# The third matrix of each expert in 16 KB runs, and up products that read every second pair of columns

## The chip, the cores and the metric

The kernel runs on one core of a Trainium2 chip. The time is that of one execution on the device, in microseconds (us), and the median of three runs is what is compared. The engines of the core are TensorE (PE; its weight loads are shown apart as PEld), VectorE (DVE), ScalarE (ACT), GpSimd (POOL) and SyncE (SP), which here issues most of the large loads. Sixteen DMA engines move data between the device's memory and the core's on-chip memory of 128 partitions.

## What is computed

One layer of a streaming encoder for 512 prompt frames and 32 frames of a running stream, 544 tokens in all: a mixer (attention and a gated delta rule), and behind it a mixture of 32 experts, of which each token takes two. The change touches the experts alone:

```python
N_EXPERTS, TOP_K, D_MODEL, D_EXPERT = 32, 2, 1024, 512
def run_block(args):
    tok, e, wt = args
    xb = x_pad[tok]
    h = jax.nn.silu(xb @ w_e1[e]) * (xb @ w_e3[e])      # 1024 x 512 each
    return (h @ w_e2[e]) * wt[:, None].astype(xb.dtype)  # 512 x 1024
```

All matrices are float32, so that each of the three is 2 MB and an expert is 6 MB.

## The kernel before, in words

The mixer comes first and takes some 740 us. The experts follow, in `expert_blocks`: one block for each of the 32 experts, each of up to 64 tokens (`SLOTS`). Tokens lie in slots; `fetch` (GpSimd) gathers their rows for a later block, `scatter` (GpSimd) writes the block's results to a table in device memory (`choice_rows`). Behind the last block the results are read back (`load_rows`, L2619, tile `y_rows`), weighted and added by VectorE (L2821, L2829) and stored.

**One block on TensorE** is `products`. `turn` transposes the gathered rows. Then for each of the first and the third matrix of the reference (`w_e1`, `w_e3`; slots `k.w1`, `k.w3`), eight steps over the 1024 inputs, two products in each (L2543): the array's columns are split in two halves of 64, and half `a` computes 256 of the 512 hidden columns for all 64 tokens. The tokens are the stationary operand, 256 columns of the matrix are the moving one. A float32 product shows as two records in the trace, so a block has 64 of them on this line, 32 for each matrix. VectorE multiplies silu of the one with the other into `hm` (L2577), TensorE transposes `hm` in two pieces, its even and its odd columns (`hm[:, c:FH:2]`, L2548), VectorE copies the result (`hT`, L2580), and L2555 multiplies with `w_e2` in four steps of 512 columns for each half.

**How the hidden columns are dealt** decides which rows of `w_e2` each partition must hold. Before, half `a` of the array takes the hidden columns 256a to 256a + 255, side by side. Behind the transposes partition n holds the columns 2n and 2n + 1 of the first half, and 256 + 2n and 257 + 2n of the second. So `load_down` (L2160) loads two runs of two rows to each partition, 8 KB each.

**How weights arrive.** Each matrix has a ring of three slots (`RING`). Two experts and then a third are loaded while the mixer ends; in the block loop `loads` (L2582 on) issues on SP, for the expert three blocks on: the first matrix when this block's products with it are done (`first`), the other one of the pair when its products are done (`up`), the down matrix when the down products are done (`down`). All go into one queue, q1. TensorE waits for each matrix before it is used.

Nothing else sets the order: each engine's program is written out by hand, with semaphores, and blocks 6 to 29 are in a loop in which each engine does the same for three blocks.

Of the kernel before, what the change touches and what calls it, by code (L numbers as in the profile page):

```python
# [147 lines left out]
def build(nc, ins, outs):  # L148
    k = Kernel(nc, ins, outs)
    k.chains = {}  # L150
    with k.top:
# [61 lines left out]
        with ExitStack() as k.experts, ExitStack() as k.rings, ExitStack() as k.routing:  # L213
            expert_tensors(k)
            k.run(project_and_choose)
            k.routing.close()
            k.run(expert_blocks)
# [1926 lines left out]
def expert_matrix(k, name, e):  # L2144
    src = k.i[name]
    return src[0, e] if isinstance(e, int) else src[0, bass.ds(e, 1)].rearrange("o r n -> (o r) n")


def load_weights(k, sp, name, tiles, loaded, e, slot):

    src = expert_matrix(k, name, e).rearrange("(p k) n -> p (k n)", p=128)
    sp.dma_start(tiles[slot][:].rearrange("p k n -> p (k n)"), src).then_inc(loaded[slot], 16)
# [6 lines left out]

def load_down(k, sp, e, slot):  # L2160

    src = expert_matrix(k, "w_e2", e).rearrange("(a p b) n -> p a (b n)", a=2, p=128)
    sp.dma_start(k.w2[slot][:].rearrange("p (a b) n -> p a (b n)", a=2), src).then_inc(k.w2_loaded[slot], 16)


def project_and_choose(k):
# [21 lines left out]
    with nc.Block() as block:  # L2188
        @block.sync
        def _(sp):  # L2190
            for j in (2 * KD - 2, 2 * KD - 1):
                o.load(sp, j)
            sp.wait_ge(padded, 2)
            load_router(k, sp)
            for e in range(RING - 1):
                load_up(k, sp, e, e)
                load_down(k, sp, e, e)
            sp.wait_ge(projected, 2)
            load_weights(k, sp, "w_e1", k.w1, k.w1_loaded, RING - 1, RING - 1)
            sp.wait_ge(projected, 4)  # L2200
            load_weights(k, sp, "w_e3", k.w3, k.w3_loaded, RING - 1, RING - 1)
            sp.wait_ge(projected, 5)
            load_down(k, sp, RING - 1, RING - 1)
# [237 lines left out]
def expert_blocks(k):  # L2441
# [4 lines left out]
    nc = k.nc  # L2446
    V = nc.vector
    FH, NF = FE // 2, FE // 128
    STEPS, EARLY = NE // RING, 2 * RING
    further = -(-NT // SLOTS)  # L2450
    with ExitStack() as ctx:
# [4 lines left out]
        xT = k.sb("b_xT", [128, KD, SLOTS], F32, ctx)  # L2456
# [26 lines left out]
        sl = (lo, hi)  # L2483
# [3 lines left out]
        def wait(eng, sem, value):  # L2487

            if not isinstance(value, int) or value > 0:
                eng.wait_ge(sem, value)  # L2490
# [23 lines left out]
        def turn(pe, b, slot, n):  # L2514
            pe.wait_ge(gathered[slot], 16 * n + 16)
            wait(pe, copied, 2 * b)

            nc.tensor.matmul(X[0][:, 0:64], xg[lo, slot, 0:128], k.ident[lo, lo], start=True, stop=True)  # L2518
            nc.tensor.transpose(X[1][:, 0:64], xg[hi, slot, 0:128], k.ident[hi, hi])
            for d in range(1, 4):  # L2520
                for a in range(2):
                    last = nc.tensor.transpose(X[a][:, 64 * d:64 * d + 64], xg[sl[a], slot, 128 * d:128 * d + 128],  # L2522
                                               k.ident[sl[a], sl[a]])
            return last

        def place_first(pe):
# [3 lines left out]
            last.then_inc(placed, 1)  # L2530
            pe.wait_ge(joined, 1)

        def products(pe, b, slot, n, prev):
            turn(pe, b, slot, n).then_inc(turned, 1)
            pe.wait_ge(copied, 2 * b + 1)
            wait(pe, hidden, b)
            for bank, w, loaded, made in ((1, k.w1, k.w1_loaded, first), (2, k.w3, k.w3_loaded, up)):
                pe.wait_ge(loaded[slot], 16 * n + 16)
                for d in range(KD):
                    if bank == 1 and d == 4:  # L2540
                        pe.wait_ge(copied, 2 * b + 2)
                    for a in range(2):
                        last = nc.tensor.matmul(k.bank[bank][sl[a], 0:FH], xT[:, d, :], w[slot][:, d, FH * a:FH * a + FH],  # L2543
                                                start=(d == 0), stop=(d == KD - 1))
                last.then_inc(made, 1)
            pe.wait_ge(hidden, b + 1)
            for c in range(2):
                last = nc.tensor.transpose(k.bank[3][:, 128 * c:128 * c + 128], hm[:, c:FH:2], k.ident[:])  # L2548
            last.then_inc(hturned, 1)
            pe.wait_ge(hcopied, b + 1)  # L2550
            pe.wait_ge(k.w2_loaded[slot], 16 * n + 16)
            wait(pe, out, b)
            for f in range(NF):
                for a in range(2):
                    last = nc.tensor.matmul(k.bank[4][sl[a], :], hT[:, f % 2, sl[f // 2]],  # L2555
                                            k.w2[slot][:, f, 512 * a:512 * a + 512], start=(f == 0), stop=(f == NF - 1))
            last.then_inc(down, 1)
# [24 lines left out]
        def loads(sp, e, b, slot, prev):  # L2582
            sp.wait_ge(first, prev + 1)
            load_weights(k, sp, "w_e1", k.w1, k.w1_loaded, e, slot)
            sp.wait_ge(up, prev + 1)
            load_weights(k, sp, "w_e3", k.w3, k.w3_loaded, e, slot)
            sp.wait_ge(down, prev + 1)
            load_down(k, sp, e, slot)
# [34 lines left out]
        with nc.Block() as block:  # L2623
# [61 lines left out]
            @block.tensor  # L2685
            def _(pe):
                def beside(b):
                    if b == NE - 2:
                        pe.wait_ge(last_made, 1)
                        for t, (c0, n) in enumerate(TILES):  # L2690
                            place = k.bank[6][:, 128 * (t - 1):128 * t] if t else k.bank[7][:, 0:NS]
                            last = nc.tensor.transpose(place, last_oh[0:n, t, :], k.ident[0:n, 0:n])
                        last.then_inc(last_turned, 1)
                    if b != 4:
                        return
                    pe.wait_ge(coded, 1)
                    for m in range(10):
                        j = m // 5
                        last = nc.tensor.matmul(M[:, MORE * j:MORE * j + MORE], r1[:, m, :], b1[:, m, :],
                                                start=(m == 0), stop=(m == 9))  # L2700
                    last.then_inc(listed, 1)

                place_first(pe)
                n = run_blocks(pe, products, beside)
                pe.wait_ge(last_kept, 1)
                pe.wait_ge(out, n + NE)
                for m, t in enumerate(ORDER):
                    rows = TILES[t][1]
                    if m == 4:
                        pe.wait_ge(finished, 2)  # L2710
                    for a in range(2):
                        last = nc.tensor.matmul(END[m][a][0:rows, :], last_rows[sl[a], t, 0:rows], y[sl[a], (NE - 1) % RING, :],
                                                start=True, stop=True)
                    last.then_inc(last_in, 1)
# [142 lines left out]
```

## Time and profile before

| | us |
|---|---|
| median of three runs | 1228.68 |
| lowest and highest run | 1225.5, 1230.6 |
| the profiled execution | 1229.07 |
| its span, first to last instruction | 1227.3 |
| TensorE busy with products | 1090.4 (89%) |
| VectorE, ScalarE, GpSimd busy | 430.4, 354.9, 389.0 |
| moved by DMA | 284.58 MB, of it 244.94 MB on queue q1 |
| granted TensorE clock, mean | 0.958 |

TensorE is busy for 89% of the span, but that is a mean over the mixer and the experts, and the two have different limits. The page's strip of 40 slices shows the DMA engines at 20 to 70% up to 660 us, and at 90% or more, with 424 to 429 GB/s, from 767 us to almost the end. Shares of the whole run thus don't say what an edit in the experts is worth; the stretch from 740 us on has to be read by itself.

### The profile page before, as it was taken

How to read it: one execution, taken by the hardware profiler on the slowest of the kernel's cores; microseconds unless marked ns; L12 is line 12 of the kernel's file. 1: busy time of each engine (PE TensorE's matmuls, PEld its weight loads, DVE VectorE, ACT ScalarE, POOL GpSimd, SP SyncE). 2: the span in 40 equal slices, each digit the busy share in tenths (PEclk: the TensorE clock that was granted, in tenths of full speed). 3: DMA queues.
4: the chain of work that ended last, by engine and by line, in shares of the span. 5: the costliest groups of instructions: out<-in, count | busy, mean ns of one | idle time of the engine just before them, and what ended most of it. 6: DMA issues, size and time to landing. Idle time of an engine off the chain costs nothing. (4 is left out here: it accounts for less than half of the span.)

```text
span 1227.3 us, 20556 instructions
## 1 busy us (share of the span) xinstructions
PE 1090.4 (89%) x8243; PEld 834.8 (68%) x8243; DVE 430.4 (35%) x987; ACT 354.9 (29%) x749; POOL 389.0 (32%) x426
## 2 busy tenths in 40 slices
PE   5999899899999989999999898888888888777884
PEld 4998888798998868888898764454444444444441
DVE  6697733881111454331333442321111111111116
ACT  6547634352222735543332531000000000000000
POOL 4554468841212442332563102112121122111100
PEclk9999999898999989999999877998999999999997
DMA  7332236255322611115331985999999999999996
GB/s 130 87 87 61 69 93 170 43 171 142 91 69 71 222 55 52 53 49 183 93 95 36 369 323 214 427 426 429 426 428 429 427 428 429 427 427 429 429 428 263
DMA packets 149146, 284.58 MB, mean 232 GB/s; under 512 B 43588, under 2 KB 118948, under 8 KB 132688
## 3 DMA queue, kind: packets, MB, share of 16 engines
q1 hardware_dynamic: 93696, 244.94, 51.5%
q10 hardware_dynamic: 49632, 27.46, 8.3%
q0 software_dynamic: 5744, 11.15, 2.4%
q8 instruction: 51, 0.84, 0.3%
q14 instruction: 23, 0.19, 0.0%
HBM read 267.08 MB, written 24.31 MB: 237 GB/s over the span
## 5 line engine op out<-in xcount | busy, mean ns | idle before, releaser
L2543 PE MATMUL bank<-e_w,b_xT 128*64 128x256 f32 x2048 | 236.1, 388 | 33.2 <-DMA e_w<-in_w_e 17.6
L490 PE MATMUL bank<-xhi,cv_w_hi 128*128 128x272 f32 x848 | 258.1, 304 | 8.3 <-PEq L134 2.6
L476 POOL TENSOR_TENSOR cv_w_lo<-cv_w_raw,cv_w_hi 128x1024 fp32r<-128x1024 f32 (+1 forms) x69 | 166.8, 2418 | 305.8 <-ACT cv_w_hi L469 289.6
L490 PE MATMUL bank<-xhi,cv_w_lo 128*128 128x272 f32 x848 | 249.0, 294 | 0.0
L490 PE MATMUL bank<-xlo,cv_w_hi 128*128 128x272 f32 x848 | 248.4, 293 | 0.0
L2543 PEld LDWEIGHTS bank<-e_w,b_xT 128*64 128x64 f32 x2048 | 149.6, 139 | 109.6 <-DVE b_xT L2572 26.2
L490 PEld LDWEIGHTS bank<-xhi,cv_w_hi 128*128 128x128 f32 x848 | 163.7, 193 | 17.0 <-issue 9.7
L490 PEld LDWEIGHTS bank<-xlo,cv_w_hi 128*128 128x128 f32 x848 | 164.1, 194 | 1.1
L490 PEld LDWEIGHTS bank<-xhi,cv_w_lo 128*128 128x128 f32 x848 | 163.8, 193 | 0.0
L2555 PE MATMUL bank<-e_w,b_hiddenT 128*64 128x512 f32 x512 | 118.6, 605 | 20.7 <-DVE b_hiddenT L2580 20.7
L2507 POOL COPY b_target<-slot_target 128x1 int32 (+1 forms) x31 | 5.6, 180 | 327.3 <-ACT b_y L2565 327.3
L2565 ACT ACTIVATE b_y<-bank 128x512 f32<-128x512 f32 x32 | 19.1, 597 | 286.5 <-PE bank L2555 286.5
L2577 DVE TENSOR_TENSOR b_hidden<-b_silu,bank 128x256 f32<-128x256 f32 x32 | 13.5, 422 | 243.5 <-issue 233.7
L2555 PEld LDWEIGHTS bank<-e_w,b_hiddenT 128*64 128x64 f32 x512 | 36.9, 138 | 80.4 <-issue 53.9
L469 ACT ACTIVATE cv_w_hi<-cv_w_raw 128x1024 fp32r<-128x1024 f32 (+1 forms) x69 | 69.3, 1004 | 28.4 <-DMA cv_w_raw<-in_w_br_a 16.5
L2572 DVE TENSOR_TENSOR b_xT<-bank,g_ffn_runs 128x256 f32<-128x256 f32 x64 | 24.2, 419 | 129.0 <-PE bank L2522 128.1
L678 DVE SCALAR_TENSOR_TENSOR conv_acc<-conv_in,wconv,conv_acc 128x547 f32<-128x547 f32 x48 | 60.5, 1261 | 1.7
L2562 ACT ACTIVATE b_silu<-bank 128x256 f32<-128x256 f32 x32 | 12.3, 383 | 144.2 <-PE bank L2543 144.2
L2075 PE MATMUL bank<-o_hi,mix_prompt 128*128 128x512 f32 x128 | 44.3, 411 | 1.4 <-PEq L134 0.7
L490 PE MATMUL bank<-yb_hi,cv_w_hi 128*128 128x272 f32 x128 | 41.4, 324 | 1.4 <-DVE yb_lo L1648 1.4
L490 PE MATMUL bank<-yb_lo,cv_w_hi 128*128 128x272 f32 x128 | 38.4, 300 | 0.0
L490 PE MATMUL bank<-yb_hi,cv_w_lo 128*128 128x272 f32 x128 | 38.4, 300 | 0.0
(447 smaller groups left out, 1650.7 us busy)
## 6 DMA issues: line engine op xcount, KB each, us to landing
e_w<-in_w_e SPq DMA_DIRECT2D x96, 2048.0 KB, 28.9
cv_w_raw<-in_w_in ACTq DMA_DIRECT2D x34, 512.0 KB, 4.1
cv_w_raw<-in_w_in SPq DMA_DIRECT2D x18, 512.0 KB, 3.9
cv_w_raw<-in_w_br_b ACTq DMA_DIRECT2D x8, 512.0 KB, 4.2
o_raw<-in_w_out SPq DMA_DIRECT2D x16, 256.0 KB, 3.6
y_rows<-choice_rows SPq DMA_DIRECT2D x8, 512.0 KB, 7.3
g_values_gates<-g_z_stage ACTq DMA_DIRECT2D x12, 272.0 KB, 4.6
f_gates<-g_values_gates SPq DMA_DIRECT2D x2, 1088.0 KB, 11.1
```

What stands on the lines that cost most here:

```text
L469: self.k.nc.scalar.activation(self.whi[:, c % OPS, 0:nk, :], self.raw[:, c % RAWS, 0:nk, :], ACT.Copy)\
L476: self.k.nc.gpsimd.tensor_tensor(self.wlo[:, s, 0:nk, :], self.raw[:, s, 0:nk, :], self.whi[:, c % OPS, 0:nk, :].bitcast(F32), ALU.subtract)\
L490: last = self.k.nc.tensor.matmul(self.bank(c, h)[:, 0:HALF], w, x[:, d, cols], start=(d == 0 and n == 0), stop=(d == nk - 1 and n == 2))
L678: op = nc.vector.scalar_tensor_tensor(out=ac[:, 0:W], in0=ci[:, w:w + W], scalar=k.wconv[:, w, c:c + 1], in1=ac[:, 0:W], op0=ALU.mult, op1 ...
L2075: last = k.nc.tensor.matmul(bank[0:n, :], rows, w[:, d, :], start=(start and i == 0), stop=(d == KD - 1 and i == 2))
L2507: nc.gpsimd.tensor_copy(to[:, slot:slot + 1], k.dst[:, bass.ds(column, 1)]).then_inc(aimed, 1)
L2543: last = nc.tensor.matmul(k.bank[bank][sl[a], 0:FH], xT[:, d, :], w[slot][:, d, FH * a:FH * a + FH], start=(d == 0), stop=(d == KD - 1))
L2555: last = nc.tensor.matmul(k.bank[4][sl[a], :], hT[:, f % 2, sl[f // 2]], k.w2[slot][:, f, 512 * a:512 * a + 512], start=(f == 0), stop=(f ...
L2562: nc.scalar.activation(act[:], k.bank[1][:, 0:FH], ACT.Silu).then_inc(silu, 1)
L2565: nc.scalar.activation(y[:, slot, :], k.bank[4][:], ACT.Copy).then_inc(out, 1)
L2572: nc.vector.tensor_tensor(xT[:, f], X[a][:, 0:4 * SLOTS].rearrange("p (k s) -> p k s", k=4), k.gain[:, f].unsqueeze(2).broadcast_to([128, ...
L2577: nc.vector.tensor_tensor(hm[:], act[:], k.bank[2][:, 0:FH], ALU.mult).then_inc(hidden, 1)
```

## The change

Two things that belong together. Half `a` of the array no longer takes 256 hidden columns side by side, but the columns 4n + 2a and 4n + 2a + 1 for each n from 0 to 127: pairs, dealt to the halves in turn. The moving operand of L2543 is read with a step for that: two floats (8 bytes), then two left out. The number of columns, of products and of steps is the same. Behind the transposes partition n then holds the hidden columns 4n to 4n + 3, so that its rows of `w_e2` are four neighbours, one run of 16 KB, and `load_down` becomes the same call as for the other two matrices.

```diff
 def load_down(k, sp, e, slot):

-    src = expert_matrix(k, "w_e2", e).rearrange("(a p b) n -> p a (b n)", a=2, p=128)
-    sp.dma_start(k.w2[slot][:].rearrange("p (a b) n -> p a (b n)", a=2), src).then_inc(k.w2_loaded[slot], 16)
+    load_weights(k, sp, "w_e2", k.w2, k.w2_loaded, e, slot)
...
+        def pairs_of(row, a):
+
+            return row.rearrange("p (n f) -> p n f", f=NF)[:, :, 2 * a:2 * a + 2]
+
...
-                        last = nc.tensor.matmul(k.bank[bank][sl[a], 0:FH], xT[:, d, :], w[slot][:, d, FH * a:FH * a + FH],
+                        last = nc.tensor.matmul(k.bank[bank][sl[a], 0:FH], xT[:, d, :], pairs_of(w[slot][:, d, :], a),
                                                 start=(d == 0), stop=(d == KD - 1))
```

No instruction moves to another place. On SP, at the place where the first loads of expert weights are issued (the end of the mixer; `e_w_0_8390`, `8391` and `8392` are the first, third and down matrix of ring slot 0, the next three those of slot 1), the change reads:

```order
 L2152 DMA e_w_0_8390<-in_w_e 128x4096
 L2152 DMA e_w_0_8391<-in_w_e 128x4096
-L2163 DMA e_w_0_8392<-in_w_e 128x2x2048
+L2152 DMA e_w_0_8392<-in_w_e 128x4096
 L2152 DMA e_w_1_8393<-in_w_e 128x4096
 L2152 DMA e_w_1_8394<-in_w_e 128x4096
-L2163 DMA e_w_1_8395<-in_w_e 128x2x2048
+L2152 DMA e_w_1_8395<-in_w_e 128x4096
 L2152 DMA e_w_2_8396<-in_w_e 128x4096 [waits g_last]
```

The down load keeps its place and its waits and loses a dimension of its pattern. The other engines' programs read alike but for line numbers.

## Rows read from the trace of the kernel before

**Rows 1.** The chain that ended last: start us, us, what; the first blocks.

```profile
744.20 9.98 PE bank L2543 x64
...
760.56 3.70 PE bank L2543 x32
...
774.08 3.70 PE bank L2543 x32
```

**Rows 2.** The same chain later, up to its end.

```profile
983.83 3.70 PE bank L2543 x32
...
997.29 3.70 PE bank L2543 x32
1001.14 37.77 DMA e_w<-in_w_e
...
1039.05 3.69 PE bank L2543 x32
1042.89 42.20 DMA e_w<-in_w_e
...
1085.23 3.69 PE bank L2543 x32
...
1177.67 3.69 PE bank L2543 x32
...
1181.77 4.50 issue
...
1193.19 6.55 DMA choice_rows<-b_y,b_target
...
1203.78 10.64 DMA y_rows<-choice_rows
```

**Rows 3.** Windows: stretch, length, busy (count) by engine, PEclk, DMA share, GB/s.

```profile
770.00:1000.00 230.00, 200.72 (x1525) 108.42 (x1523) 38.77 (x110) 16.28 (x33) 47.95 (x102) 0.99 1.01 427
1000.00:1180.00 180.00, 145.36 (x1092) 81.69 (x1090) 19.21 (x48) 11.76 (x24) 31.93 (x67) 0.99 1.01 428
```

**Rows 4.** DMA queues, whole run: packets, MB, share of 16 engines' time.

```profile
q1 hardware_dynamic: 93696, 244.94, 51.5%
```

**Rows 5.** The same queue from 1000 to 1180 us alone.

```profile
q1 hardware_dynamic: 6534, 73.92, 96.4%
```

**Rows 6.** Line L2163, the down loads: ns min/median/max of the issue.

```profile
L2163 SPq DMA_DIRECT2D e_w<-in_w_e x32: 378/384/4415, 677.7 to 1161.5; - x32
```

**Rows 7.** Timeline of TensorE: one block while the ring is ahead.

```profile
916.54 7.13 PE L2543 MATMUL bank<-e_w,b_xT 128*64 128x256 f32 x64 [0.53 <-DVE b_xT L2572]
```

**Rows 8.** Timeline late: products with idle time before them and releaser.

```profile
1177.67 3.67 PE L2543 MATMUL bank<-e_w,b_xT 128*64 128x256 f32 x32 [0.74 <-DMA e_w<-in_w_e]
...
1182.49 3.67 PE L2543 MATMUL bank<-e_w,b_xT 128*64 128x256 f32 x32 [1.15 <-DMA e_w<-in_w_e]
...
1193.45 3.67 PE L2543 MATMUL bank<-e_w,b_xT 128*64 128x256 f32 x32 [0.61 <-DVE b_xT L2572]
```

**Rows 9.** Timeline at 62 us: mixer products, float32r, contiguous moving operand.

```profile
62.04 0.29 PE L490 MATMUL bank<-xhi,cv_w_hi 128*128 128x272 f32 x1
62.16 0.29 PE L490 MATMUL bank<-xlo,cv_w_hi 128*128 128x272 f32 x1
62.29 0.29 PE L490 MATMUL bank<-xhi,cv_w_lo 128*128 128x272 f32 x1
```

**Rows 10.** Weight loads of lines L2548 and L2699: ns min/median/max.

```profile
L2548 PEld LDWEIGHTS bank<-ident,b_hidden x64: 194/205/219, 754.8 to 1202.0; 128*128 128x128 f32 x64
...
L2699 PEld LDWEIGHTS bank<-m_blk_oh,m_rank_oh x20: 186/192/192, 813.4 to 815.5; 128*128 128x128 f32 x20
```

**Rows 11.** Line L2510, the 31 scatters: issue to landing.

```profile
DMA to landing us min/median/max: 6.5/7.8/8.9
```

**Rows 12.** A window in which the stream ran fastest: TensorE columns, PEclk, DMA share, GB/s.

```profile
1043.80:1047.50 3.70, 3.63 (x32) 2.21 (x32) 1.00 1.06 440
```

## The prediction

> **What bounds the kernel now.** I read the chain that ended last first, since the engines' shares mix the mixer with the experts. Both edits lie behind 740 us. In the first blocks the chain goes through TensorE and the small copies beside it alone: the products of block 1 start at 760.56, of block 2 at 774.08 [rows 1], and and blocks 17 and 18 at 983.83 and 997.29, a period of 13.46 us [rows 2]. In this stretch TensorE doesn't wait for weights, because three experts were loaded before it began. From block 18 on the chain is different: the products with one matrix (3.69 us) and then 42.20 us of a weight load, over and over [rows 2]. A load is issued when its slot comes free and lands 42 us later, since eight other matrices stand ahead of it in the queue. Blocks 21 and 30 start at 1039.05 and 1177.67, so nine blocks take 138.6 us, 15.40 us each [rows 2].
>
> The windows then say why: the DMA engines are at a share of 1.01, with 427 GB/s, from 770 to 1000 us already, and at 428 GB/s from 1000 to 1180 [rows 3]. The stream of weights is full from the first released slot on; TensorE, at 13.46 us a block, only lives on the lead of the ring until block 18. Check: q1 moves 73.92 MB in 180 us [rows 5], which is 0.411 MB/us, and an expert's 6.29 MB take 15.3 us by that, which is the 15.40 of the chain. So **the experts' stretch is bound by the bytes and packets of the weight stream**, and behind it by a short tail: the last but one block's results go out (6.55 us) and everything is read back (10.64 us) [rows 2].
>
> TensorE's reserve is needed below. From 997.29 thirteen more blocks at 13.46 us would start block 31 at 1172.3; it starts at 1193.45 [rows 8]. So TensorE has 21.2 us in hand by then, 0.68 us a block over 31 blocks, and 1.9 us a block (15.40 less 13.46) once the lead is used up.
>
> **The change, part one: the down loads in packets of 16 KB.** The bytes stay the same. An 8 KB run is a packet, and so is a 16 KB run: a down matrix goes from 256 packets to 128, for each of 16 DMA engines from 16 to 8. What is a packet worth beyond its bytes? Two rows of the same queue give it. The whole run: 51.5% of 16 x 1227.3 us are 10113 engine-us for 244.94 MB in 93696 packets [rows 4]. The full stretch: 96.4% of 16 x 180 us are 2776 engine-us for 73.92 MB in 6534 packets [rows 5]. With a price per MB and one per packet, both rows hold for 36.4 us per MB and 12.7 ns per packet. The many small packets of the mixer (writes, and copies within device memory) carry costs of their own, so 12.7 ns is an upper end; the lower end is 0. The queue is fully busy by its share, so I see no reason for a loss here. I take the middle, 6.4 ns, as neither row shows a 16 KB packet by itself.
>
> On the path: 8 packets x 6.4 ns are 0.05 us for a down load. The chain's last load ahead of the tail is that for block 30 (TensorE idle 1.15 us before 1182.49, released by a load [rows 8]); ahead of it in the full stretch stand the down loads of experts 3 to 29, 27 of them. The five others lie before 740 us or behind. **27 x 0.05 = 1.4 us less**, and between 0 and 27 x 0.10 = 2.7 us less. The gain is not taken by what comes next: TensorE needs 13.46 us a block and would get weights each 15.35 us.
>
> The Trainium skill ("DMA: Bandwidth & Descriptors", section "Why small descriptors are slow (HBM only)") puts a fixed cost of about 3 cycles on each packet, and gives 850 MHz for the fabric. An estimate by that page is 3.5 ns a packet and 0.8 us in all; no row here shows a packet's fixed part alone.
>
> SP's own share is nothing: a down load is issued in 384 ns [rows 6] against 15.40 us a block, and nothing queued behind it on SP is late by that.
>
> **Part two: moving columns read with a step.** 1024 records on each of the two matrices' lines now read two floats of every four. The trace has no moving operand with a step, so this needs bounds. From below: nothing, or a gain of nothing, since the same columns are streamed. From above: twice the time. Three rows speak to where between. Contiguous products of 272 columns start every 0.126 us in the mixer [rows 9], 0.46 ns a column. The up products of one matrix take 3.67 us [rows 8] for 32 records of 256 columns, two at a time by the halves of the array, so 4096 columns in each stream: 0.90 ns a column. If the step halves the pace at which columns can be read, to 0.93 ns, a stream that needs 0.90 loses 3%. That holds if a column is read once for its record and not once per pass over it; if it is read twice, the stream already runs at the full pace and the step would double it. The third row is of the weight side: L2548 loads every second float, so also two of four, at 205 ns, and L2699 the same size without a step at 192 ns [rows 10]: 7% more, not 100%. I go by that row, the nearest with a step: at most 7% of 7.13 us [rows 7], 0.5 us a block. That is less than the 0.68 us a block in hand, so it costs nothing before the tail. In the tail the second half of block 30's products is on the chain, 0.25 us; I round it to nothing and keep it in the range.
>
> The Trainium skill ("SBUF — State Buffer", section "Specifications (TRN2)") says that lines of the memory are 16 bytes, that two hits per line are wanted for full bandwidth, and that each cross to a new line pays a penalty. Pairs are two hits, so by its first half the sum stays as it is. By its second half, twice as many lines are crossed, which would speak for the slow rival below. The 205 against 192 ns is as near as a row here comes to it.
>
> **Part three: what larger packets do to others.** Gathers and scatters share the DMA engines with the weights. A small packet behind a 16 KB one waits 0.6 us (16.4 KB at 36.4 us per MB), behind an 8 KB one 0.3 us. That can only matter for the last scatter, which is on the chain at 6.55 us [rows 2] and partly beside the last down load. The 31 scatters land after 6.5 to 8.9 us [rows 11], and this one is at the short end, so the worst is 2.4 us more. I take nothing, as the pair before it in the queue is unchanged, and keep 2.4 us for the range.
>
> **Sum.** 1229.07 (the profiled execution; span 1227.3 and 1.8 around it) less 1.4 is 1227.7. The profiled execution is 0.4 us above the median of the runs, so in terms of the median: 1228.7 - 1.4 = **1227.3 us**. A difference of under 0.5% (6 us) can hardly be told from no change by a measurement of this kernel, so I expect no change that can be seen.
>
> **Rivals.** (a) *The step makes TensorE the bound.* For it: nothing in the trace shows a moving operand with a step, and the two passes may each read the columns. Against it: 205 to 192 ns on the weight side. It decides from 0.68 us a block, about 10% on the products. If they double (7.13 us has 6.9 us of streaming), a block takes 20.4 us, 31 blocks x (6.9 - 0.68) = 193 us come on top, and some 4 us in the tail: about 1425 us. At 25% more (1.75 us) it would be 33 us, about 1260. The DMA share from 770 to 1180 us would then fall well below 1. (b) *The stream gets faster by more than a packet's price*, because the 8 KB runs hold it up in a way that my two rows don't separate. The best stretch of 3.7 us ran at 440 GB/s [rows 12] against 428. Had all of the 430 us of the full stretch this rate, they would shrink by 2.7%, 12 us: 1217. Against it: the share is 1.01 already, and short windows swing by where packets end. (c) *The read-back tail loses more than the stream gains*: 2.4 us for the last scatter and 0.3 for the products, against 0: 1231.4. (d) *The loads stay as they were* because packets are cut at 8 KB anyway. Against it: q1's bytes per packet in the full stretch, 73.92 MB over 6534, are 11.3 KB, above 8. It gives 1228.7.
>
> **How the numbers follow.** Forecast 0.70, (c) 0.09, (d) 0.05, all of these within 0.5%; (a) 0.09, slower; (b) 0.05, faster; 0.01 each for a fast and a slow end that I have not named. So faster 0.06, same 0.84, slower 0.10. The range: below, 1228.7 less 2.7 and less the 3.2 us by which runs lie under the median, 1223; above, rival (c) and the 1.9 us by which they lie over it, 1233. It leaves (a) and (b) out, 0.16 with the rest.
>
> **What would show each step.** q1 should have 4096 packets less. The windows should still read 1.01 and 427 to 430 GB/s. The up products of a matrix should still take 3.67 us, or 3.9 with the 7%; the nine blocks from 21 to 30 should take 138.2 us instead of 138.6. What would prove me wrong: products of over 7.8 us a block where the ring is ahead, TensorE no longer waiting for loads late, or GB/s of over 433.

## The result and the profile after

The changed kernel takes 1234.74 us (median of 20 runs, 1228.05 to 1244.45), the kernel before 1232.24 us (median of 20, 1225.5 to 1235.67). The ratio is 1.0040, with a 95% interval from 1.0024 to 1.0056: 4.9 us slower, between 3.0 and 6.9. The ratio is an estimate from all the single runs; the two medians alone lie 2.5 us apart and the two means 4.0, so the size of the loss is known only roughly, its sign well. It is no change by the bound of 0.5%, as the forecast has it, but the time lies above its range of 1223 to 1233, and the sign of the small difference is the other one.

The comparison is of 20 runs on each side, not of three. With 20, the kernel before is at 1232.24 us and not at the 1228.68 from which the prediction started; that alone is 3.6 us, and the last section comes back to it.

| | before | after |
|---|---|---|
| profiled execution, us | 1229.07 | 1233.75 |
| its span, us | 1227.3 | 1232.0 |
| granted TensorE clock | 0.958 | 0.957 |

**The stream did what was forecast.** The queue's row of the whole run has 4096 packets less than [rows 4]:

```profile
q1 hardware_dynamic: 89600, 244.94, 51.1%
```

From 1000 to 1180 us the same queue, against 6534 packets and 96.4% [rows 5], and the two windows (columns as in [rows 3]):

```profile
q1 hardware_dynamic: 5066, 73.81, 96.0%
```

```profile
770.00:1000.00 230.00, 201.33 (x1478) 105.28 (x1476) 38.62 (x112) 15.70 (x32) 46.26 (x97) 0.98 1.01 428
1000.00:1180.00 180.00, 153.88 (x1138) 80.17 (x1134) 20.06 (x50) 11.78 (x24) 32.36 (x69) 1.00 1.01 429
```

The share stays at 1.01 and the rate goes up by 1 GB/s in both windows.

**The stepped read has a price, and it is hidden.** The line of the up products, once as its own row (ns min/median/max) and once late in the timeline with the idle time before it:

```profile
L2546 PE MATMUL bank<-e_w,b_xT x2048: 385/388/689, 748.4 to 1204.5; 128*64 128x256 f32 x187
```

```profile
1166.21 3.84 PE L2546 MATMUL bank<-e_w,b_xT 128*64 128x256 f32 x32 [0.84 <-DVE b_xT L2575]
...
1197.03 3.85 PE L2546 MATMUL bank<-e_w,b_xT 128*64 128x256 f32 x32 [0.61 <-DVE b_xT L2575]
```

3.84 us for 32 records stand against 3.67 [rows 8]: 5%. The chain shows where it goes:

```profile
981.50 3.87 PE bank L2546 x32
...
995.30 3.87 PE bank L2546 x32
...
1078.10 7.49 PE bank L2546 x64
1085.61 38.90 DMA e_w<-in_w_e
...
1128.43 37.75 DMA e_w<-in_w_e
...
1196.78 8.01 DMA choice_rows<-b_y,b_target
...
1208.52 10.59 DMA y_rows<-choice_rows
```

A block takes 13.80 us while TensorE sets the pace, against 13.46 [rows 2]. So TensorE lives on the ring's lead longer, until 1085.61 us instead of 1001.14, and then waits for loads as before. The last blocks come at the pace of the stream in both.

**What is new at the end** is the last scatter: 8.01 us against 6.55 us [rows 2].

**What is new at the start** lies in a stretch of which the prediction showed no row, the end of the mixer. There GpSimd stores the normalised token rows (`c_xn` into `token_rows`), ScalarE makes the next 128 rows when the store before has landed, and GpSimd gathers the first expert's rows (`c_first_idx`) when all of them are there. These stores share the DMA engines with the nine loads of the first three experts. GpSimd's timeline of the kernel before (idle time before a row, and who ended it, in brackets):

```profile
685.70 0.82 POOL L2228 DMA_DIRECT2D token_rows<-c_xn  x1 [8.13 <-ACT c_xn L2269]
699.00 0.56 POOL L2228 DMA_DIRECT2D token_rows<-c_xn  x1 [12.48 <-ACT c_xn L2269]
711.40 0.53 POOL L2228 DMA_DIRECT2D token_rows<-c_xn  x1 [11.83 <-ACT c_xn L2269]
725.25 0.53 POOL L2228 DMA_DIRECT2D token_rows<-c_xn  x1 [13.32 <-ACT c_xn L2269]
734.26 1.11 POOL L2224 DMA_INDIRECT b_rows<-token_rows,c_first_idx  x1 [8.48 <-DMA token_rows<-c_xn]
```

and of the changed one:

```profile
688.20 0.81 POOL L2227 DMA_DIRECT2D token_rows<-c_xn  x1 [8.45 <-ACT c_xn L2268]
702.99 0.56 POOL L2227 DMA_DIRECT2D token_rows<-c_xn  x1 [13.98 <-ACT c_xn L2268]
...
738.65 1.11 POOL L2223 DMA_INDIRECT b_rows<-token_rows,c_first_idx  x1 [10.31 <-DMA token_rows<-c_xn]
```

SP issues the first weight load just ahead of them, at 676.72 us before and at 679.16 after:

```profile
676.72 0.91 SPq L2152 DMA_DIRECT2D e_w<-in_w_e  x2
```

```profile
679.16 3.19 SPq L2152 DMA_DIRECT2D e_w<-in_w_e  x6
```

The program up to there is the same in both, and over the twelve other traces of this study that moment lies anywhere from 677.9 to 688.7 us. So stretches are measured from it: **the gather comes 57.54 us behind the first weight load before, and 59.49 after.**

The 4.7 us between the two spans then close: 2.44 lie before the first weight load and are no matter of the change; 1.95 between it and the gather; from the gather to the last scatter's issue 458.93 us before (1193.19 less 734.26) and 458.13 after (1196.78 less 738.65), 0.80 less, most of it in the blocks (0.6); the scatter 1.46 more; the read-back 0.35 less. Sum 4.70.

### The profile page after: what moved, and what is told of

Same layout as the page of the kernel before. It is cut to its first block and busy times, and to the rows that moved or that the text cites. A ratio compares the mean times of both kernels' runs of the same rounds, so it can differ in the third digit from the quotient of the medians.

```text
span 1232.0 us, 20556 instructions
## 1 busy us (share of the span) xinstructions
PE 1100.2 (89%) x8243; PEld 830.4 (67%) x8243; DVE 435.3 (35%) x987; ACT 355.4 (29%) x749; POOL 389.0 (32%) x426
## 3 DMA queue, kind: packets, MB, share of 16 engines
q1 hardware_dynamic: 89600, 244.94, 51.1%
## 5 line engine op out<-in xcount | busy, mean ns | idle before, releaser
L2546 PE MATMUL bank<-e_w,b_xT 128*64 128x256 f32 x2048 | 247.5, 398 | 26.3 <-DVE b_xT L2575 20.7
L2546 PEld LDWEIGHTS bank<-e_w,b_xT 128*64 128x64 f32 x2048 | 147.1, 138 | 115.9 <-DVE b_xT L2575 25.8
L2565 ACT ACTIVATE b_silu<-bank 128x256 f32<-128x256 f32 x32 | 12.3, 384 | 150.5 <-PE bank L2546 150.5
```

The lines of the kernel that those rows point to most:

```text
L2565: nc.scalar.activation(act[:], k.bank[1][:, 0:FH], ACT.Silu).then_inc(silu, 1)
```

## The experiments

In all of them three things are read from the same rows as above: W (the first weight load's issue), G (the gather by `c_first_idx`) and the last scatter. The ratios are to runs of the kernel before that were taken beside them. Two theories stood at the start. P: the small loss comes from the stepped read. Q: it comes from the larger packets, which delay the small transfers of other queues.

### One part alone

**The step alone**: the change without its load.

```diff
 def load_down(k, sp, e, slot):
-    load_weights(k, sp, "w_e2", k.w2, k.w2_loaded, e, slot)
+    src = expert_matrix(k, "w_e2", e).rearrange("(a p b) n -> p a (b n)", a=2, p=128)
+    sp.dma_start(k.w2[slot][:].rearrange("p (a b) n -> p a (b n)", a=2), src).then_inc(k.w2_loaded[slot], 16)
```

> The changed kernel with the down loads of before (two runs of 8 KB, so the rows of the down matrix don't fit the order of the hidden columns; the output differs for that, the work is the same). Theory P (the step costs): the products of one matrix take 3.84 us instead of 3.67, and the whole difference of the change, +4 us (ratio 1.003 to 1.004), is in this kernel. Theory Q (the packets cost, at the end of the mixer and in the last scatter): the 3.84 us are there too, but hidden behind the weight stream, and the time is within 1 us of before (ratio 0.999 to 1.001); the last gather of the mixer's end waits 8.5 to 9 us for the token rows, as before, and the last scatter lands after 6.5 us.

Measured: ratio 0.9998 (0.9980 to 1.0016), the median 1229.86 us against 1231.29 for the kernel before beside it. Its products and block period are those of the changed kernel, and the gather is as early as before:

```profile
979.03 3.87 PE bank L2547 x32
...
992.83 3.88 PE bank L2547 x32
...
1197.02 6.61 DMA choice_rows<-b_y,b_target
```

```profile
739.59 1.11 POOL L2224 DMA_INDIRECT b_rows<-token_rows,c_first_idx  x1 [9.05 <-DMA token_rows<-c_xn]
```

13.80 us a block, G 56.95 us behind its W of 682.64, the scatter in 6.61 us. The step costs nothing that shows in the whole time: theory P falls.

**The runs alone**: the kernel before with one line of the change.

```diff
 def load_down(k, sp, e, slot):
-    src = expert_matrix(k, "w_e2", e).rearrange("(a p b) n -> p a (b n)", a=2, p=128)
-    sp.dma_start(k.w2[slot][:].rearrange("p (a b) n -> p a (b n)", a=2), src).then_inc(k.w2_loaded[slot], 16)
+    load_weights(k, sp, "w_e2", k.w2, k.w2_loaded, e, slot)
```

> The kernel before with every down load in 16 KB runs (the rows of the down matrix don't fit the order of the hidden columns; the output differs, the work is the same). Theory Q: the store of token rows ahead of the last gather of the mixer's end takes 10.5 us or more instead of 9, the last scatter 8 instead of 6.5, the stream gives back 1 to 1.5; together +2 to +3 us (ratio 1.002). Theory P: nothing but the gain of the stream, -1.4 us (ratio 0.999).

Measured: ratio 1.0043 (1.0018 to 1.0068), as much as the whole change. The expected 1.002 lies near the low end of that.

```profile
746.19 1.11 POOL L2223 DMA_INDIRECT b_rows<-token_rows,c_first_idx  x1 [9.59 <-DMA token_rows<-c_xn]
```

```profile
1202.74 8.15 DMA choice_rows<-b_y,b_target
```

G lies 59.90 us behind its W of 686.29, and the scatter takes 8.15. Q holds so far. Which of the packets do it?

### Which packets

The same line, once for the down loads of the first three experts alone and once for the 29 others alone.

```diff
+def load_down_whole(k, sp, e, slot):
+
+    load_weights(k, sp, "w_e2", k.w2, k.w2_loaded, e, slot)
...
-                load_down(k, sp, e, e)
+                load_down_whole(k, sp, e, e)
...
-            load_down(k, sp, RING - 1, RING - 1)
+            load_down_whole(k, sp, RING - 1, RING - 1)
```

> The kernel before with the down loads of the first three experts alone in 16 KB runs (their rows don't fit the order of the hidden columns, so the output differs). Theory Q: +1.5 to +2 us, all of it before the first up product of the experts. Theory P: no change (ratio 0.999 to 1.001).

```diff
             sp.wait_ge(down, prev + 1)
-            load_down(k, sp, e, slot)
+            load_down_whole(k, sp, e, slot)
```

> The kernel before with the down loads of experts 3 to 31 in 16 KB runs and the first three as before (rows of experts 3 to 31 don't fit, so the output differs). Both theories give the stream's gain of about 1.4 us by block 30; theory Q takes it back in the last scatter (8 us instead of 6.5), so the time is that of before within 0.5 us; theory P gives 1.4 us less (ratio 0.999).

Measured for the first three: 1.0047 (1.0027 to 1.0067), which is 5.8 us (3.3 to 8.3) and so more than the 1.5 to 2 us expected. For the others: 1.0001 (0.9979 to 1.0022). The gather and the last scatter of the one and of the other:

```profile
742.39 1.11 POOL L2229 DMA_INDIRECT b_rows<-token_rows,c_first_idx  x1 [10.26 <-DMA token_rows<-c_xn]
```

```profile
1201.30 6.58 DMA choice_rows<-b_y,b_target
```

```profile
739.30 1.11 POOL L2229 DMA_INDIRECT b_rows<-token_rows,c_first_idx  x1 [8.70 <-DMA token_rows<-c_xn]
```

```profile
1195.90 8.04 DMA choice_rows<-b_y,b_target
```

Three of the 96 weight loads carry the whole visible loss: G is 60.12 us behind W (682.27) in the first, 56.49 (682.81) in the second. The other 29 down loads bring the scatter's 1.4 us and take 0.8 us off the stream, which leaves 0.6 us, too little to be seen.

### The step at its worst

Half `a` reads the columns 4n + 2a for all n first, then the columns 4n + 2a + 1: one float of every four at a time instead of two. The sets of hidden columns stay the same, and the transposes behind take their columns side by side.

```diff
-            return row.rearrange("p (n f) -> p n f", f=NF)[:, :, 2 * a:2 * a + 2]
+            return row.rearrange("p (n f) -> p f n", f=NF)[:, 2 * a:2 * a + 2, :]
...
-                last = nc.tensor.transpose(k.bank[3][:, 128 * c:128 * c + 128], hm[:, c:FH:2], k.ident[:])
+                last = nc.tensor.transpose(k.bank[3][:, 128 * c:128 * c + 128], hm[:, 128 * c:128 * c + 128], k.ident[:])
```

> The changed kernel with the hidden columns dealt in single floats: half a reads the columns 4n + 2a, then the columns 4n + 2a + 1, so each float read comes from another 16 bytes; hidden lies in halves of 128, and the transposes in front of the down products read it without a step. Output as the reference. If the pace of a stepped read goes by how many floats of each 16 bytes are taken (two of four cost 5%: 3.84 instead of 3.67 us for a matrix), one of four costs much more: up to double, 7 us, by which a block takes over 20 us and the time is over 1400 us. If the step costs a fixed time per product (0.17 us over 32 records, 5 ns each), it stays at 3.84 us and the time is that of the changed kernel, 1232 to 1236 us.

Measured: 1444.87 us, ratio 1.174 (1.170 to 1.179). Its timeline, and the window from 800 to 1400 us:

```profile
900.32 14.70 PE L2546 MATMUL bank<-e_w,b_xT 128*64 128x256 f32 x64 [0.53 <-DVE b_xT L2575]
921.28 14.64 PE L2546 MATMUL bank<-e_w,b_xT 128*64 128x256 f32 x64 [0.53 <-DVE b_xT L2575]
```

```profile
800.00:1400.00 600.00, 550.69 (x2602) 194.47 (x2600) 56.67 (x150) 27.45 (x56) 77.09 (x163) 0.99 0.81 296
```

The products of a block take 14.70 us, twice the 7.13 of [rows 7]; the period is 20.96 us and the DMA share falls to 0.81. This is rival (a), which the prediction priced at 1425 us, with the condition that it did not know: one float of four doubles the time, two of four add 5%.

This trace shows something about the mixer's end too, where its weight loads are those of the changed kernel. TensorE's granted clock was 0.60 from 726 to 730 us, its products there were late, and with them the load that waits for them, the third expert's down load: SP issued it at 731.84 us, 1.3 us behind the fourth store of token rows, where the changed kernel issues the two within 0.1 us. The DMA engines were nearly idle just before (a share of 0.06 from 726 to 730 us), and the fourth store landed 2.9 us after its issue, where it takes 9.2 to 9.9 us in the five other traces with 16 KB packets. G then waited for VectorE:

```profile
730.52 0.53 POOL L2227 DMA_DIRECT2D token_rows<-c_xn  x1 [11.96 <-ACT c_xn L2268]
738.72 1.11 POOL L2223 DMA_INDIRECT b_rows<-token_rows,c_first_idx  x1 [7.66 <-DVE c_first_idx L2430]
```

### Smaller packets instead

If larger packets delay the mixer's end, smaller ones should speed it up. Here the nine loads of the first three experts are cut in four, so that a packet is 4 KB; all later loads stay as they are. The waits for weights count 48 further, for the three more pieces of each slot's first load. The first is the changed kernel so cut, the second the kernel before.

```diff
+def load_pieces(k, sp, name, tiles, loaded, e, slot):
+
+    rows = tiles[slot].shape[1]
+    src = expert_matrix(k, name, e).rearrange("(p k) n -> p k n", p=128)
+    for j in range(0, rows, rows // PIECES):
+        sp.dma_start(tiles[slot][:, j:j + rows // PIECES, :], src[:, j:j + rows // PIECES, :]).then_inc(loaded[slot], 16)
...
-    load_weights(k, sp, "w_e1", k.w1, k.w1_loaded, e, slot)
-    load_weights(k, sp, "w_e3", k.w3, k.w3_loaded, e, slot)
+    load_pieces(k, sp, "w_e1", k.w1, k.w1_loaded, e, slot)
+    load_pieces(k, sp, "w_e3", k.w3, k.w3_loaded, e, slot)
```

> The changed kernel with all nine loads of the first three experts cut in four (one quarter of each partition's run per load: packets of 4 KB instead of 16 KB). Output as the reference. Theory Q (a store's packet waits behind one weight packet of whatever size): the end of the mixer, from the first weight load's issue to the issue of the last gather, takes 54 us or less instead of 59.5 (57.0 before), and the whole run 1227 or less. Theory R (the stores share the bytes evenly whatever the packets' size, and the 2.8 us have another reason): 59 us, and the time of the changed kernel, 1234.

> The kernel before with the same nine loads cut in four, packets of 4 KB. Output as the reference. Theory Q: as the changed kernel with pieces, at most 1 us from it, 1226 to 1228 us; the mixer's end takes 54 us or less. Theory R: no change, 1231 us.

Measured: 1225.85 us, ratio 0.9968 (0.9942 to 0.9993), and 1227.33 us, 0.9971 (0.9950 to 0.9992), both against the kernel before at 1230.99 us beside them. The gather of the first and of the second:

```profile
730.52 1.11 POOL L2233 DMA_INDIRECT b_rows<-token_rows,c_first_idx  x1 [12.44 <-DVE c_first_idx L2440]
```

```profile
736.57 1.15 POOL L2241 DMA_INDIRECT b_rows<-token_rows,c_first_idx  x1 [11.96 <-DVE c_first_idx L2448]
```

G is 52.67 and 52.49 us behind W (677.85 and 684.08). The releaser has changed: the gather waits for its indices from VectorE and no longer for a store. ScalarE's waits for the stores are almost gone too. Of the four that the kernel before has (2.1 to 8.0 us), one of 0.26 us is left in the first of the two, and two of 0.48 and 0.69 us in the second. The first's:

```profile
715.19 2.07 ACT L2278 ACTIVATE c_xn<-x_rows,c_rms 128x1024 f32<-128x1024 f32 x1 [0.26 <-DMA token_rows<-c_xn]
```

With the gather bound by VectorE, smaller packets than these could gain nothing more there. The next version cuts the last expert's three loads in four as well, so that the last scatter lies beside 4 KB packets.

```diff
+        def last_loads(sp, e, b, slot, prev):
+            sp.wait_ge(first, prev + 1)
+            load_pieces(k, sp, "w_e1", k.w1, k.w1_loaded, e, slot)
+            sp.wait_ge(up, prev + 1)
+            load_pieces(k, sp, "w_e3", k.w3, k.w3_loaded, e, slot)
+            sp.wait_ge(down, prev + 1)
+            load_pieces(k, sp, "w_e2", k.w2, k.w2_loaded, e, slot)
```

> The changed kernel with packets of 4 KB for the first three experts and for the last one (its third and down matrix are what the last scatter meets). Output as the reference. Theory Q: the last scatter lands after 6 us or less instead of 8, so the time is 1.5 to 2 us below the kernel with the first three alone. Theory R: the scatter stays at 8 us.

Measured: 1228.76 us, 0.9971 (0.9950 to 0.9991), G 52.69 us behind W. The last scatter of it and of the version that leaves the last expert alone:

```profile
1192.61 6.64 DMA choice_rows<-b_y,b_target
```

```profile
1186.88 8.06 DMA choice_rows<-b_y,b_target
```

The scatter goes back to 6.64 us, not to 6 or less as expected: from 16 KB packets beside it to smaller ones it gains 1.4, but 4 KB are no better for it than the 6.6 us that 8 KB give. The packet records of the trace show where it stops: the scatter's rows themselves follow each other faster (1.8 us from the first to the last, against 2.6 in the kernel before and 3.6 in the changed one), but the first of them starts 3.9 us behind the issue, where it takes 2.5 to 3.4 us in the twelve others. Why it starts late in this one trace is open. Nor is the whole faster than without this edit; 1.4 us is less than these intervals resolve.

### One packet of the weights for each row

What the stores wait for can be counted. Here are the two queues (q1 the weight loads, q0 GpSimd's) from the first to the last row of the first store, in the kernel before (690.23 to 694.04 us, beside 8 KB packets), in the changed kernel (692.44 to 698.42, beside 16 KB), and of the second store in the changed kernel in pieces (702.11 to 704.64, beside 4 KB): packets, MB, share of 16 engines.

```profile
q1 hardware_dynamic: 134, 1.08, 68.3%
q0 software_dynamic: 131, 0.52, 33.4%
```

```profile
q1 hardware_dynamic: 139, 2.02, 80.2%
q0 software_dynamic: 137, 0.52, 21.2%
```

```profile
q1 hardware_dynamic: 150, 0.54, 52.5%
q0 software_dynamic: 133, 0.52, 50.3%
```

Without the packets of a few bytes that these rows count as well, 128 rows of the store go beside 132, 123 and 131 packets of weights: one for each row, whatever its size. With 128 rows on 16 engines, an engine has eight rows of 4 KB in turn. At 36.4 us per MB a row takes 0.15 us, a packet of weights 0.15, 0.3 or 0.6 us, so eight pairs take 2.4, 3.6 and 6.0 us; the three stretches are 2.5, 3.8 and 6.0 us long. This is the form of theory Q that the pieces were to test, and theory R (even shares of the bytes) falls.

It also says which stores the change can reach. From issue to landing, in us, means over the five traces with 8 KB and the same five with 16 KB as in the table below, without the single floats:

| store | 8 KB | 16 KB | difference |
|---|---|---|---|
| first | 10.1 | 12.0 | +1.9 |
| second | 10.0 | 11.1 | +1.1 |
| third | 11.4 | 10.0 | -1.4 |
| fourth | 7.8 | 9.7 | +1.9 |

The first, second and fourth go beside down loads. The third goes beside the third expert's other two matrices, whose packets have 16 KB in the kernel before as well (130 of them between its first and last row there, none of 8 KB), so it can't get slower; it gets faster, as in four of the five traces with 16 KB fewer packets are left beside it (65 to 92, against 127 to 150). Together the four make 3.5 us.

### Both kernels again

Three traces on each side showed G less W at 56.5 to 57.5 us with 8 KB packets and at 59.5 to 60.1 with 16 KB. A fourth with 16 KB, that of the single floats, has 58.06, for the reason given there; the expectations below leave it out. Each kernel was traced twice more, without an edit, to see how much of that is scatter between executions, and whether another difference goes with it: from G to the first `b_silu` (the first block's first activation) some traces had 14.5 us and some 16.4.

> The kernel before once more, for one look. Theory Q (the packets of the first three experts' down loads delay the token rows' stores): from the first weight load's issue to the last of the choosing step's gathers (c_first_idx) 57.0 us, within 0.6, as in the three traces with 8 KB packets there (57.5, 57.0, 56.5); the last scatter in 6.6 us. If the 2.8 us between the groups were scatter between executions, this one could read 59 or more. From that gather to the first b_silu the traces so far show either 14.5 to 14.8 us or 16.4. If that went with the packets too, the kernel before should read 14.5 in most executions and the changed one 16.4; if it is the place at which TensorE's granted clock comes back to 1.0, either kernel can show either, with the products of the first block at 0.5 or 1.0 beside it.

> The changed kernel once more, for one look. Theory Q: from the first weight load's issue to the gather 59.8 us, within 0.6, as in the three traces with 16 KB packets there (59.5, 59.9, 60.1); the last scatter in 8.0 us. From the gather to the first b_silu: 16.4 if that goes with the packets, 14.5 or 16.4 if it is only the moment at which the granted clock returns.

> As r1_before: 57.0 us within 0.6 up to the gather and 6.6 us for the last scatter by theory Q; 59 or more in one of the two looks would speak against it. Gather to first b_silu 14.5 in both by the packets, either by the clock's moment.

> As r2_after: 59.8 us within 0.6 up to the gather and 8.0 us for the last scatter by theory Q; 58 or less would speak against it. Gather to first b_silu 16.4 in both by the packets, either by the clock's moment.

All traces together, in us (the stretch from first to last `b_silu`, block 0 to block 31, is mostly the stream's; TensorE's slower products bind the single floats there, so that row is left open):

| kernel | first down loads | later ones | G less W | G to first `b_silu` | first to last `b_silu` | last scatter |
|---|---|---|---|---|---|---|
| before | 8 KB | 8 KB | 57.54 | 16.5 | 446.5 | 6.55 |
| step alone | 8 KB | 8 KB | 56.95 | 14.5 | 447.1 | 6.61 |
| before, again | 8 KB | 8 KB | 56.42 | 14.5 | 446.5 | 6.61 |
| before, again | 8 KB | 8 KB | 55.97 | 14.7 | 446.9 | 6.86 |
| runs in the 29 others | 8 KB | 16 KB | 56.49 | 14.6 | 446.1 | 8.04 |
| runs in the first three | 16 KB | 8 KB | 60.12 | 16.4 | 446.6 | 6.58 |
| after | 16 KB | 16 KB | 59.49 | 16.5 | 445.9 | 8.01 |
| runs alone | 16 KB | 16 KB | 59.90 | 14.8 | 445.8 | 8.15 |
| after, again | 16 KB | 16 KB | 60.54 | 15.0 | 446.0 | 7.84 |
| after, again | 16 KB | 16 KB | 61.14 | 16.4 | 445.8 | 8.03 |
| single floats | 16 KB | 16 KB | 58.06 | - | - | - |
| before, in pieces | 4 KB | 8 KB | 52.49 | 14.5 | 446.5 | 6.62 |
| after, in pieces | 4 KB | 16 KB | 52.67 | 14.6 | 446.0 | 8.06 |
| both ends in pieces | 4 KB | 16 KB, the last expert 4 KB | 52.69 | 14.6 | 446.4 | 6.64 |

The expected 57.0 and 59.8 within 0.6 were missed by two of the four (55.97 and 61.14), but away from each other: the five traces with 8 KB (mean 56.67) and the five with 16 KB (mean 60.24) don't touch, 3.6 us apart. With the single floats the 16 KB side starts at 58.06, still above the 57.54 of the other. The scatter goes by the packets of the later loads without an exception, 6.6 to 6.9 us beside 8 KB and 7.8 to 8.2 beside 16 KB; the stretch between the first and the last `b_silu` is 446.7 in the mean with 8 KB and 445.9 with 16 KB (the version with both ends in pieces apart).

The stretch from the gather to the first `b_silu` didn't split that way: 16.4 us or near it in three of these five with 16 KB, in one of five with 8 KB, in none with 4 KB. What differs inside is TensorE's granted clock. In the profiled execution of the changed kernel, at 16.4 us, the first products of the experts run at 0.50 to 0.52 for a long while (the last three numbers are the granted clock, the DMA share and GB/s):

```profile
746.65:750.65 4.00, 2.91 (x21) 1.75 (x20) 1.92 (x10) 1.60 (x3) 1.41 (x3) 0.50 0.14 38
750.65:754.65 4.00, 4.00 (x22) 2.19 (x20) 0.00 (x0) 0.00 (x0) 0.00 (x0) 0.52 0.11 29
```

that is at 1.2 GHz. The traces at 14.5 to 15.0 us read 0.85 to 0.94 in the window at the same distance from the gather (12 to 16 us), as this one of the step alone:

```profile
751.59:755.59 4.00, 4.00 (x36) 2.42 (x34) 0.00 (x0) 0.39 (x1) 0.00 (x0) 0.94 0.34 54
```

TensorE's wait ahead of this doesn't decide it: the kernel before, at 16.5 us, had waited 0.86 us for the gather's stage, the runs alone, at 14.8 us, 5.47. Whether later gathers make the slower case more frequent can't be said from three against one.

## Why the prediction was wrong

**Held.** The packets (4096 less), the windows (1.01, 428 and 429 GB/s), the up products (3.84 us, under the 3.9 of the 7% bound) and the cover for them: 0.34 us a block is less than the 0.68 in hand, and the step alone measures 0.9998. That the weight side's 7% was the row to go by, against twice the time, came out near, at 5%; no run shows that the two have the same cause, so the nearness may be luck. The Trainium skill's rule for the memory ("SBUF — State Buffer", section "Specifications (TRN2)"), two hits for each 16 byte line, fits both cases: with two floats of each line the products take 5% longer, with one twice as long. The second half of that rule, a penalty for each line crossed, may be the 5%; no run parts the two halves.

**The base.** The forecast of 1227.3 us is 7.4 us below the 1234.74 measured. Of these, 3.6 are the base: 1228.68 was the median of three runs, and that of 20 is 1232.24. The gain of 1.4 that was forecast and didn't come, and the 2.5 by which the two medians differ, make the rest. From 1232.24 the same range would have ended at 1236.6 us and held the measured time, with the sign still wrong; and from 1228.68 the true mechanism, 4.2 us as summed below, would just have stayed inside it, at 1232.9.

**Part one, right in sign, too large in size.** The prediction took 6.4 ns for a packet and 1.4 us in all. The stretch from the first to the last `b_silu` shrinks by 0.8 us (446.7 to 445.9), over the 28 down loads of experts 3 to 30: 28 x 8 packets, 3.4 ns each. The estimate by the Trainium skill ("DMA: Bandwidth & Descriptors", section "Why small descriptors are slow (HBM only)"), 3.5 ns and 0.8 us, was the better one; the upper bound from [rows 4, 5] had pulled the middle up.

**Part one, the step that failed:** "The five others lie before 740 us or behind", and with that they were costed at nothing. Three of those five loads lie before 740 us, and they are the expensive ones: 3.6 us between the first weight load and the gather, and the pair of runs that changes these three alone (1.0047) and all but these three (1.0001) shows that the loss goes with them. What the prediction said of the queue, that it is fully busy and so nothing is lost, is true of the queue and not of those who share its engines. No row ahead of the prediction shows the stores between 677 and 740 us.

**Part three, the second step:** "That can only matter for the last scatter", and there "I take nothing, as the pair before it in the queue is unchanged". It did matter for that scatter, by 1.4 us (6.64 to 8.02 in the means), inside the bound of 2.4 us. And it was not the only transfer on the chain: the token rows' stores were the other, in rows of 4 KB on GpSimd's queue. The prediction's own price, 0.3 us more for each packet that is waited for, is right, and it lacked the count: one packet for each row, eight rows in turn, 2.4 us for a store that is beside down loads from its first row to its last. The first store is (1.9 us measured), the second and the fourth are in part (1.1 and 1.9), the third isn't. For the scatter the queue's records have 58 packets of data and not 128 (32 of 4 KB and 26 of 2 KB), about four in turn on an engine, 1.2 us by the same price.

The Trainium skill ("DMA: Bandwidth & Descriptors", section "Queues, rings and completion order") says that each DMA engine goes round its queues a packet at a time. The counts above agree if a run of the weights is such a packet and a row of the store another. That section of the Trainium skill calls 9 to 17 descriptors a typical packet; the counts here, one run for one row, show no such grouping.

**The new sum.** 3.6 at the mixer's end and 1.4 in the scatter, less 0.8 in the stream: 4.2 us, with 4.9 (3.0 to 6.9) measured. The same terms give 4.2 for the runs alone (5.3 measured, 2.2 to 8.4), 3.6 for the first three loads (5.8, 3.3 to 8.3) and 0.6 for the others (0.1, 2.6 less to 2.7 more): all inside, if on the low side for two. The slow clock at the first block may add part of 1.9 us in some executions; that is left open. Rival (c), with 2.4 us for the scatter, was nearest, and its mechanism was half of the answer.

## What to carry to other kernels

- When a stream's packets change size, look for everybody else's small transfers beside it, on any queue, and ask who waits for each: a full queue hides its own packet price but not what it does to others. Multiply the change of a packet's time by the rows that an engine has to move for the small transfer, and look in the trace whether the large packets are beside it for all of its rows.
- Take the base of a forecast from as many runs as its size asks for: here the median of three lay 3.6 us off that of 20, as much as the effect itself.
- A saving that repeats 29 times beside a full stream can be worth less than three of its copies at the hand-over between stages, so cost the first and the last copies by their own rows. Here the largest packets were the worst choice beside the stores: 4 KB packets in the first nine loads gave 0.9968, against 1.0040 for the change alone.
- Where an engine has time in hand, a stepped float32 operand can be cheap: two neighbouring floats of every four cost 5% here, one of every four twice the time. Other steps weren't tried.

## What the runs showed of the hardware

- TensorE, float32, moving operand of 256 columns, two products side by side: 3.67 us for 32 records side by side in memory, 3.84 with two floats of every four (5% more), 14.70 us for 64 records with one of every four, against 7.13 side by side (twice).
- A contiguous 16 KB run goes as one packet: 89600 against 93696 in the whole run. A packet less was worth 3.4 ns (0.8 us over 224 packets an engine), as far as two groups of traces 0.8 us apart can say.
- A store of 128 rows of 4 KB, issued by GpSimd beside SP's weight loads, has one packet of the weights for each of its rows, of whatever size: 2.5 us from the first row to the last beside 4 KB packets, 3.8 beside 8 KB, 6.0 beside 16 KB. With the DMA engines idle ahead of it, such a store landed 2.9 us after its issue; beside the weight loads it took 6.8 to 12.3.
- Over four such stores, from the first weight load to the gather behind them: 52.6 us with 4 KB packets (where VectorE is the releaser), 56.7 with down loads of 8 KB, 60.2 with 16 KB throughout.
- The last scatter, 58 packets of 2 and 4 KB: 6.6 us beside 4 and 8 KB packets, 8.0 beside 16 KB.
